# A feed-forward stage in token blocks of 848, 848 and 416 instead of three of 704

## The chip, the cores and the metric

The kernel runs on one core of a Trainium2 chip. The metric is the device time of one execution in microseconds, the median of several runs. One core has TensorE (PE; its weight loads are PEld), VectorE (DVE), ScalarE (ACT), GpSimd (POOL), SyncE (SP, which here only issues transfers) and 16 DMA engines.

## The reference

One layer of a streaming encoder in float32, for 2048 prompt frames and 64 decoder frames of width 1024 (2112 tokens): a projection, two kinds of banded attention, an output projection with a residual, and then the part that matters here:

```python
def conv_ffn(h, conv_state, w_gate_up, conv_w, conv_b, w_down):
    gate, up = jnp.split(jnp.einsum("bsd,df->bsf", h, w_gate_up), 2, axis=-1)   # d = 1024, f = 2816
    ext = jnp.concatenate([conv_state, gate], axis=1)     # two rows of state ahead
    conv = conv_b
    for i in range(3):
        conv = conv + conv_w[i] * ext[:, i:i + t]
    y = jax.nn.silu(conv) * up
    return jnp.einsum("bsf,fd->bsd", y, w_down), ext[:, -2:]
# x = x + conv_ffn(RMSNorm(x)), for the prompt with zero state, for the decoder frames with theirs
```

## The kernel before

Four stages follow each other, with a barrier between: `project`, `attend`, `combine` (output projection, residual x1T and normed input h2T, both to DRAM) and `ffn` (L1413). Only `ffn` is touched. In it the 2112 tokens are columns of the moving operand, in N_BLOCKS = 3 blocks of BLOCK = 704, each cut in SUBS = 2 chunks of SUB = 352. The decoder's 64 tokens are the last columns of the last block; CUT is the column of that block where the prompt ends.

**Precision.** Every float32 operand is split in a hi and a lo part, and `dense` (L74) makes three matmuls for each tile of the contraction: hi x hi, lo x hi, hi x lo. The weights, which are stationary, are split here too: ScalarE copies w_raw to w_hi (`split_hi`, L1580), VectorE subtracts to w_lo (`split_lo`, L1639). Each of the two slots s has one buffer of w_raw, w_hi and w_lo. SyncE refills w_raw (`load_pair`, L1476) as soon as `split_lo` has read it; `split_hi` waits until TensorE has used the old weights (`z_ok[s]` of the slot's last chunk), and TensorE waits for `w_lo_ok[s]`.

**Order.** For each block the 2816 hidden channels come in PARTS = 2 parts. A part has KF = 11 gate/up pairs and then DOWN = 4 down pairs. A gate/up pair has slot 0 for a gate tile and slot 1 for the up tile of the same 128 channels, each with 8 contraction tiles; a down pair has two output tiles with 11 contraction tiles each. A group is what one slot does for one chunk: 8 x 3 = 24 or 11 x 3 = 33 matmuls into z[s][j]. TensorE's order (`pair`, L1550) is slot 0 chunk 0, slot 0 chunk 1, slot 1 chunk 0, slot 1 chunk 1.

**Gate and up.** ScalarE copies z[0][j] to `gate` (L1600), splits the next gate weights, then makes silu of both chunks and splits the next up weights. VectorE (`gate_up`, L1663) copies the two carried columns ahead, convolves each chunk in three operations (`convolve`, L1652, into c1, with c2 between), in the last block also the decoder's 64 columns with their own state (L1675 to L1682), then makes w_lo of slot 0, then for each chunk y = silu x z[1][j] and its hi and lo parts (L1690 to L1695), then w_lo of slot 1. In `down` it adds z to the residual tile acc.

**Between blocks.** In the down pairs of part 1, ScalarE makes h_hi of the next block and POOL h_lo (`split_h`, L1509) from tiles that POOL loads; POOL also stores yT and then loads the next acc. TensorE waits for POOL's eight tiles ahead of a block (L1562). Only for the first block SyncE loads h (into acc, L1486), ScalarE makes h_hi, and VectorE h_lo (L1646); TensorE's first group waits for these tile by tile (L1567).

Of the kernel before, what the change touches and what calls it, by code (L numbers as in the profile page):

```python
# [1412 lines left out]
def ffn(nc, h2T, x1T, w_gu, w_dn, conv, state, yT, gate_prompt, gate_sample):  # L1413
# [10 lines left out]
    LAST = N_BLOCKS - 1  # L1424
    CUT = SEQ - LAST * BLOCK
    H = 2
    with ExitStack() as ctx:
# [15 lines left out]
        y = [m.sbuf(f"y{j}", [P, SUB]) for j in range(SUBS)]  # L1443
# [58 lines left out]
        @block.gpsimd  # L1502
        def _(pool):
            def load_h(b, k):
                if b > 1 or k > 1:
                    pool.wait_ge(p_lo_ok, KD * (b - 1) + k - 1)
                pool.dma_start(h_raw[k % 2][:], h2T[k, :, b * BLOCK:(b + 1) * BLOCK]).then_inc(h_ld[k % 2], 16)

            def split_h(b):  # L1509

                for k in range(KD):
                    n = KD * (b - 1) + k
                    pool.wait_ge(h_hi_ok, n + KD + 1)
                    nc.gpsimd.tensor_tensor(h_lo[:, k, :], h_raw[k % 2][:], h_hi[:, k, :].bitcast(F32), ALU.subtract)\
# [12 lines left out]
            load_acc(0)  # L1527
            for b in range(N_BLOCKS):
                if b < LAST:
                    load_h(b + 1, 0)  # L1530
                    load_h(b + 1, 1)
                    split_h(b + 1)
                g1 = (b * PARTS + PARTS - 1) * PAIRS + KF
                for d in range(KD):
                    for j in range(SUBS):
                        pool.wait_ge(z_free[d % 2][j], g1 + d // 2 + 1)  # L1536
                    pool.dma_start(yT[d, :, b * BLOCK:(b + 1) * BLOCK], acc[:, d, :]).then_inc(y_st, 16)  # L1537
                if b < LAST:
                    load_acc(b + 1)
            pool.wait_ge(carry_ok, N_BLOCKS * F_TILES)  # L1540
            pool.wait_ge(tail_ok, F_TILES)  # L1541
            pool.dma_start(gate_sample, carry[:]).then_inc(gate_st, 16)  # L1542
            pool.dma_start(gate_prompt, tail[:]).then_inc(gate_st, 16)  # L1543
            pool.wait_ge(gate_st, 32)
            pool.wait_ge(y_st, 16 * KD * N_BLOCKS)


        @block.tensor
        def _(pe):
            def pair(g, hi, lo, n_k, ready=None):  # L1550
                for s in range(2):
                    pe.wait_ge(w_lo_ok[s], g + 1)
                    for j in range(SUBS):
                        pe.wait_ge(z_free[s][j], g)
                        cols = slice(j * SUB, (j + 1) * SUB)
                        dense(nc, z[s][j][:, 0:SUB], (lambda k: w_hi[s][:, k, :], lambda k: w_lo[s][:, k, :]),
                              (lambda k: hi[:, k, cols], lambda k: lo[:, k, cols]), n_k,
                              ready and (lambda k: ready(s, j, k))).then_inc(z_ok[s][j], 1)

            for b in range(N_BLOCKS):  # L1560
                if b:
                    pe.wait_ge(p_lo_ok, KD * b)  # L1562
                for part in range(PARTS):
                    n = b * PARTS + part
                    g0 = n * PAIRS
                    if n == 0:
                        pair(0, h_hi, h_lo, KD, lambda s, j, k: s == j == 0 and pe.wait_ge(h_lo_ok, k + 1))  # L1567
                    with pe.Fori(1 if n == 0 else 0, KF) as i:
                        pair(g0 + i, h_hi, h_lo, KD)
                    for j in range(SUBS):  # L1570
                        pe.wait_ge(y_lo_ok[j], KF * (n + 1) - 1)
                    pair(g0 + KF, y_hi, y_lo, KF,
                         lambda s, j, k: k == KF - 1 and s == 0 and pe.wait_ge(y_lo_ok[j], KF * (n + 1)))
                    with pe.Fori(1, DOWN) as i:
                        pair(g0 + KF + i, y_hi, y_lo, KF)
# [3 lines left out]
        def _(act):  # L1579
            def split_hi(s, g, n_k):  # L1580
                act.wait_ge(w_ld[s], 16 * (g + 1))
                act.wait_ge(z_ok[s][1], g)
                nc.scalar.activation(w_hi[s][:, 0:n_k, :], w_raw[s][:, 0:n_k, :], ACT.Copy).then_inc(w_hi_ok[s], 1)  # L1583

            def split_h(b, k):
                if b == 0:
                    act.wait_ge(h0_ld[k], 16)
                    src = acc[:, k, :]
                else:
                    act.wait_ge(h_ld[k % 2], 16 * ((KD * (b - 1) + k) // 2 + 1))  # L1590
# [21 lines left out]
            split_hi(1, 0, KD)
            for b in range(N_BLOCKS):
                for part in range(PARTS):
# [23 lines left out]
        def _(dve):  # L1638
# [24 lines left out]
            def gate_up(b, g, f, c, jf, n_k):  # L1663
# [5 lines left out]
                for j in range(SUBS):  # L1669
# [3 lines left out]
                    convolve(c1[j][:, 0:n], c2[j][:, 0:n], gate[:, j * SUB:H + (j + 1) * SUB], taps, n, c,  # L1673
                             (c1_ok[j], c2_ok[j], conv_ok[j] if n == SUB else s_gate_ok))
# [9 lines left out]
                nc.vector.tensor_scalar(of(carry, f), gate[:, BLOCK:H + BLOCK], 1.0, None, ALU.mult).then_inc(carry_ok, 1)  # L1684
                for j in range(SUBS):
# [4 lines left out]
                    nc.vector.tensor_tensor(y[j][:], silu[j][:], z[1][j][:, 0:SUB], ALU.mult).then_inc(z_free[1][j], 1)  # L1690
                    dve.wait_ge(z_free[1][j], g + 1)
                    hi, lo = (ap[:, ds(jf, 1), cols].rearrange("p a n -> p (a n)") for ap in (y_hi, y_lo))
                    nc.vector.tensor_scalar(hi, y[j][:], 1.0, None, ALU.mult).then_inc(y_hi_ok[j], 1)
                    dve.wait_ge(y_hi_ok[j], c + 1)
                    nc.vector.tensor_tensor(lo, y[j][:], hi.bitcast(F32), ALU.subtract).then_inc(y_lo_ok[j], 1)  # L1695
                split_lo(1, g + 1, n_k)

            def down(g, i, n_k):
                for s in range(2):
                    for j in range(SUBS):  # L1700
                        dve.wait_ge(z_ok[s][j], g + 1)
                        part = acc[:, ds(2 * i + s, 1), j * SUB:(j + 1) * SUB].rearrange("p a n -> p (a n)")
                        nc.vector.tensor_tensor(part, part, z[s][j][:, 0:SUB], ALU.add).then_inc(z_free[s][j], 1)  # L1703
# [11 lines left out]
            for b in range(N_BLOCKS):  # L1715
                for part in range(PARTS):
# [6 lines left out]
                    with nc.vector.Fori(0, DOWN - 1) as i:  # L1723
                        down(g0 + KF + i, i, KF)
                    down(g0 + PAIRS - 1, DOWN - 1, KD if n + 1 < N_BLOCKS * PARTS else 0)
# [98 lines left out]
```

## Time and profile before

| | |
|---|---|
| three runs | 2729.56, 2730.96, 2731.3 us; median 2730.96 |
| the profiled execution | 2730.9 us, its span 2729.1 us |
| mean granted TensorE clock | 0.978 |
| PE busy, share of the span | 2604.4 us, 95% |
| DVE, ACT, POOL busy | 1376.9, 887.8, 189.9 us |
| `ffn` on TensorE | 9504 matmuls of 128x352, from 1203.00 us on |

A row of the timeline gives start, duration, engine, line, operation, tile written and tiles read, shape and count, and in brackets the idle time before it with what ended it. A matmul's duration there is that of its way through the array and overlaps the next one's, so the distance between the starts is what one costs.

### The profile page before, as it was taken

The numbers are of one execution on the slowest core, as the hardware profiler recorded it, in microseconds if no ns is written. First come the engines' busy times: TensorE is split into PE (matmuls) and PEld (weight loads), VectorE is DVE, ScalarE is ACT, GpSimd is POOL, SyncE is SP. The second block draws the span as 40 slices with busy tenths as digits, with TensorE's granted clock in tenths as the row PEclk, the third lists the DMA queues.
The fourth block names the chain that finished last, engine by engine and source line by source line (L and its number), as shares of the span: only waits on it lengthen the run. The fifth ranks groups of instructions, "written<-read, shape, count | busy, mean of one in ns | idle before, by whom it ended". The sixth has DMA issues, their size and how long they took to land.

```text
span 2729.1 us, 45154 instructions
## 1 busy us (share of the span) xinstructions
PE 2604.4 (95%) x16553; PEld 2504.4 (92%) x16553; DVE 1376.9 (50%) x2973; ACT 887.8 (33%) x1696; POOL 189.9 (7%) x125
## 2 busy tenths in 40 slices
PE   6999999589999979969999999999999999999998
PEld 3888888489999979859999999999999999999998
DVE  5544444466667645565534552554355346625651
ACT  4233332476777633232212221221122222212220
POOL 0000000332322200000000002000000210000000
PEclk8999999799999989979999999999999999999999
DMA  6232231544334165562221223322122342221221
GB/s 218 86 96 79 92 94 48 123 114 102 86 86 101 46 236 180 192 238 66 73 75 55 69 92 121 123 69 79 60 69 71 105 145 65 79 68 62 69 87 64
DMA packets 175286, 271.61 MB, mean 100 GB/s; under 512 B 19138, under 2 KB 120482, under 8 KB 175074
## 3 DMA queue, kind: packets, MB, share of 16 engines
q1 hardware_dynamic: 167842, 246.13, 29.8%
q0 software_dynamic: 4848, 23.12, 2.4%
q10 hardware_dynamic: 2512, 1.26, 0.2%
q8 instruction: 51, 0.84, 0.1%
q14 instruction: 33, 0.27, 0.0%
HBM read 216.35 MB, written 55.69 MB: 100 GB/s over the span
## 4 chain that ended last, share of the span: by engine, by line
PE 55%; DVE 0%; DMA 0%; POOL 0%; issue 0%; ACT 0%; SPq 0%; POOLq 0%
PE ffn_z L81 55%; DVE ffn_h_lo L1646 0%; DMA ffn_acc<-h2T_scratch 0%; ACT ffn_h_hi L1592 0%; POOL yT L1537 0%; POOL gate_sample L1542 0%; DVE ffn_acc L1703 0%; POOL gate_prompt L1543 0%; SPq L1488 0%; SPq L1486 0%; POOLq L1541 0%; POOLq L1536 0%
## 5 line engine op out<-in xcount | busy, mean ns | idle before, releaser
L81 PE MATMUL ffn_z<-ffn_h_hi,ffn_w_hi 128*128 128x352 f32 x2112 | 680.6, 322 | 22.1 <-DVE ffn_w_lo L1641 21.9
L81 PE MATMUL ffn_z<-ffn_h_lo,ffn_w_hi 128*128 128x352 f32 x2112 | 680.2, 322 | 0.0
L81 PE MATMUL ffn_z<-ffn_h_hi,ffn_w_lo 128*128 128x352 f32 x2112 | 680.0, 322 | 0.0
L1583 ACT ACTIVATE ffn_w_hi<-ffn_w_raw 128x1024 fp32r<-128x1024 f32 (+1 forms) x180 | 205.6, 1142 | 716.9 <-PE ffn_z L81 715.8
L81 PEld LDWEIGHTS ffn_z<-ffn_h_hi,ffn_w_hi 128*128 128x128 f32 x2112 | 397.2, 188 | 24.2 <-DVE ffn_w_lo L1641 23.0
L81 PEld LDWEIGHTS ffn_z<-ffn_h_hi,ffn_w_lo 128*128 128x128 f32 x2112 | 397.5, 188 | 0.0
L81 PEld LDWEIGHTS ffn_z<-ffn_h_lo,ffn_w_hi 128*128 128x128 f32 x2112 | 397.5, 188 | 0.0
L81 PE MATMUL ffn_z<-ffn_y_lo,ffn_w_hi 128*128 128x352 f32 x1056 | 340.0, 322 | 0.0
L81 PE MATMUL ffn_z<-ffn_y_hi,ffn_w_hi 128*128 128x352 f32 x1056 | 339.7, 322 | 0.0
L81 PE MATMUL ffn_z<-ffn_y_hi,ffn_w_lo 128*128 128x352 f32 x1056 | 339.5, 321 | 0.0
L242 PE MATMUL project_z<-project_w_hi,project_h_hi 128*128 128x512 f32 (+3 forms) x680 | 255.3, 375 | 13.0 <-DVE project_w_lo L411 12.9
L1641 DVE TENSOR_TENSOR ffn_w_lo<-ffn_w_raw,ffn_w_hi 128x1024 fp32r<-128x1024 f32 (+1 forms) x180 | 238.9, 1327 | 37.3 <-ACT ffn_w_hi L1583 37.3
L242 PE MATMUL project_z<-project_w_lo,project_h_hi 128*128 128x512 f32 (+3 forms) x680 | 251.9, 371 | 0.0
L242 PE MATMUL project_z<-project_w_hi,project_h_lo 128*128 128x512 f32 (+3 forms) x680 | 251.9, 370 | 0.0
L836 PE MATMUL attend_o<-attend_v,attend_prob_t 128*128 (+1 forms) x1680 | 222.9, 276 | 0.0
L1703 DVE TENSOR_TENSOR ffn_acc<-ffn_acc,ffn_z 128x352 f32 (+1 forms) x96 | 50.1, 522 | 342.1 <-PE ffn_z L81 342.1
L836 PEld LDWEIGHTS attend_o<-attend_v,attend_prob_t 128*128 128x128 f32 x1680 | 209.6, 193 | 0.6
L81 PEld LDWEIGHTS ffn_z<-ffn_y_hi,ffn_w_lo 128*128 128x128 f32 x1056 | 198.8, 188 | 0.0
L81 PEld LDWEIGHTS ffn_z<-ffn_y_lo,ffn_w_hi 128*128 128x128 f32 x1056 | 198.3, 188 | 0.0
L81 PEld LDWEIGHTS ffn_z<-ffn_y_hi,ffn_w_hi 128*128 128x128 f32 x1056 | 198.1, 188 | 0.0
L1600 ACT ACTIVATE ffn_gate<-ffn_z 128x352 f32<-128x352 f32 x132 | 61.6, 466 | 397.0 <-PE ffn_z L81 396.9
L1654 DVE TENSOR_SCALAR ffn_c<-ffn_gate,ffn_conv 128x352 f32<-128x352 f32 (+1 forms) x132 | 60.5, 458 | 218.7 <-ACT ffn_gate L1600 194.3
(149 smaller groups left out, 3790.8 us busy)
## 6 DMA issues: line engine op xcount, KB each, us to landing
ffn_w_raw<-w_gu SPq DMA_DIRECT2D x132, 512.0 KB, 3.6
ffn_w_raw<-w_dn SPq DMA_DIRECT2D x48, 704.0 KB, 4.1
combine_w_raw<-w_o SPq DMA_DIRECT2D x24, 512.0 KB, 4.9
combine_o_raw<-oT_scratch SPq DMA_DIRECT2D x12, 704.0 KB, 6.4
combine_x<-xT SPq DMA_DIRECT2D x12, 704.0 KB, 7.4
x1T_scratch<-combine_x SPq DMA_DIRECT2D x12, 704.0 KB, 7.5
ffn_acc<-x1T_scratch POOLq DMA_DIRECT2D x3, 2816.0 KB, 11.8
yT<-ffn_acc POOLq DMA_DIRECT2D x24, 352.0 KB
```

Source lines behind the costliest of these rows:

```text
L81: last = nc.tensor.matmul(out, w_parts[w](k), act_parts[a](k), start=(k == 0 and (w, a) == PASSES[0]), stop=(k == n_k - 1 and (w, a) == PA ...
L242: last = nc.tensor.matmul(z[c][0:w, 0:width], h[:, k, 0:w], ww[:, k, first:first + width], start=(k == 0 and h is hi and ww is w_hi), stop ...
L836: last = nc.tensor.matmul(o_ps[u % 2][:, head * P:(head + 1) * P], prob_t[u % 2][:, src:src + P], v[:, ds(tile + j, 1), pair * P:(pair + 1 ...
L1583: nc.scalar.activation(w_hi[s][:, 0:n_k, :], w_raw[s][:, 0:n_k, :], ACT.Copy).then_inc(w_hi_ok[s], 1)
L1600: nc.scalar.activation(gate[:, H + j * SUB:H + (j + 1) * SUB], z[0][j][:, 0:SUB], ACT.Copy)\
L1641: nc.vector.tensor_tensor(w_lo[s][:, 0:n_k, :], w_raw[s][:, 0:n_k, :], w_hi[s][:, 0:n_k, :].bitcast(F32), ALU.subtract).then_inc(w_lo_ok[s ...
L1654: nc.vector.tensor_scalar(dst, src[:, H:H + n], taps[:, 2:3], taps[:, 3:4], ALU.mult, ALU.add)\
L1703: nc.vector.tensor_tensor(part, part, z[s][j][:, 0:SUB], ALU.add).then_inc(z_free[s][j], 1)
```

## The change

In `ffn` alone SUB is 424 and BLOCK 848: the first two blocks have two chunks of 424, the last has REST = 416 tokens in a single chunk 0. `subs(b)` gives (index, first column, width) of a block's chunks. Every loop over chunks, every tile width and the columns of every transfer follow it. The tile y goes: it lies in c2 now, and a wait of VectorE for its own y_lo_ok stands ahead of the convolution. In the last block the prompt's convolution has CUT = 352 columns, the decoder's 64 stand behind it in the same chunk, and VectorE's `split_lo(0)` comes between the two. The other stages keep 704 and 352. The core of the diff:

```diff
+    SUB, SUBS = 424, 2
+    BLOCK = SUB * SUBS
+    REST = TOKENS - LAST * BLOCK
     CUT = SEQ - LAST * BLOCK
+    def subs(b):
+        return ((0, 0, SUB), (1, SUB, SUB)) if b < LAST else ((0, 0, REST),)
+    def cols_of(b):
+        return slice(b * BLOCK, min((b + 1) * BLOCK, TOKENS))
+    def wide(b):
+        return BLOCK if b < LAST else REST
...
-        y = [m.sbuf(f"y{j}", [P, SUB]) for j in range(SUBS)]
...
-                pool.dma_start(acc[:], x1T[:, :, b * BLOCK:(b + 1) * BLOCK].rearrange("k p n -> p k n"))\
+                pool.dma_start(acc[:, :, 0:wide(b)], x1T[:, :, cols_of(b)].rearrange("k p n -> p k n"))\
...
-            def pair(g, hi, lo, n_k, ready=None):
+            def pair(b, g, hi, lo, n_k, ready=None):
                 for s in range(2):
                     pe.wait_ge(w_lo_ok[s], g + 1)
-                    for j in range(SUBS):
+                    for j, at, width in subs(b):
                         pe.wait_ge(z_free[s][j], g)
-                        cols = slice(j * SUB, (j + 1) * SUB)
+                        cols = slice(at, at + width)
...
-            def split_hi(s, g, n_k):
+            def split_hi(b, s, g, n_k):
                 act.wait_ge(w_ld[s], 16 * (g + 1))
-                act.wait_ge(z_ok[s][1], g)
+                act.wait_ge(z_ok[s][subs(b)[-1][0]], g)
...
-                for j in range(SUBS):
+                for j, at, width in subs(b):
                     dve.wait_ge(z_free[0][j], g + 1)
                     dve.wait_ge(silu_ok[j], c)
-                    n = CUT - j * SUB if b == LAST and j else SUB
+                    dve.wait_ge(y_lo_ok[j], c)
+                    n = CUT if b == LAST else width
...
                 if b == LAST:
+                    split_lo(0, g + 1, n_k)
                     cs = c - LAST * F_TILES
                     nc.vector.tensor_scalar(gate_s[:, 0:H], of(state_sb, f), 1.0, None, ALU.mult).then_inc(s_gate_ok, 1)
-                    nc.vector.tensor_scalar(gate_s[:, H:], gate[:, H + CUT:], 1.0, None, ALU.mult).then_inc(s_gate_ok, 1)
+                    nc.vector.tensor_scalar(gate_s[:, H:], gate[:, H + CUT:H + REST], 1.0, None, ALU.mult).then_inc(s_gate_ok, 1)
                     dve.wait_ge(s_gate_ok, 3 * cs + 3)
-                    n = CUT - SUB
-                    convolve(c1[1][:, n:], c2[1][:, n:], gate_s, taps, DEC, cs, (s1_ok, s2_ok, conv_ok[1]))
+                    convolve(c1[0][:, CUT:REST], c2[0][:, CUT:REST], gate_s, taps, DEC, cs, (s1_ok, s2_ok, conv_ok[0]))
                     nc.vector.tensor_scalar(of(tail, f), gate[:, CUT:H + CUT], 1.0, None, ALU.mult).then_inc(tail_ok, 1)
-                split_lo(0, g + 1, n_k)
+                if b < LAST:
+                    split_lo(0, g + 1, n_k)
...
-                for j in range(SUBS):
-                    cols = slice(j * SUB, (j + 1) * SUB)
+                for j, at, width in subs(b):
+                    cols = slice(at, at + width)
+                    y = c2[j][:, 0:width]
                     dve.wait_ge(silu_ok[j], c + 1)
                     dve.wait_ge(z_ok[1][j], g + 1)
-                    dve.wait_ge(y_lo_ok[j], c)
```

## Rows read from the trace of the kernel before

**Rows 1.** The page, its span line.
```profile
span 2729.1 us, 45154 instructions
```

**Rows 2.** The chain that ended last, in order of time: start us, us, what.
```profile
1209.54 1510.53 PE ffn_z L81 x9483
...
2720.09 0.53 DVE ffn_acc L1703
```

**Rows 3.** Waits from 1196 us on: total us, times, longest.
```profile
PE ffn_z L81 <- DVE ffn_w_lo L1641: 21.9, 1, 21.9
```

**Rows 4.** Last block, part 1: length; busy PE PEld DVE ACT POOL; clock; DMA share, GB/s.
```profile
2467.62:2719.73 252.11, 252.11 (x1585) 252.11 (x1584) 122.95 (x265) 52.01 (x73) 3.81 (x7) 1.00 0.22 73
```

**Rows 5.** Timeline of PE: first matmuls of groups, slot 0; then a down group.
```profile
2498.18 0.32 PE L81 MATMUL ffn_z<-ffn_h_hi,ffn_w_hi 128*128 128x352 f32 x1
...
2502.02 0.32 PE L81 MATMUL ffn_z<-ffn_h_hi,ffn_w_hi 128*128 128x352 f32 x1
...
2505.82 0.32 PE L81 MATMUL ffn_z<-ffn_h_hi,ffn_w_hi 128*128 128x352 f32 x1
```
```profile
2414.99 0.32 PE L81 MATMUL ffn_z<-ffn_y_hi,ffn_w_hi 128*128 128x352 f32 x1
...
2420.30 0.32 PE L81 MATMUL ffn_z<-ffn_y_hi,ffn_w_hi 128*128 128x352 f32 x1
```

**Rows 6.** Timeline of PE in the projection, 24 matmuls of 512 apart.
```profile
252.12 0.39 PE L242 MATMUL project_z<-project_w_hi,project_h_hi 128*128 128x512 f32 x1
...
257.56 0.39 PE L242 MATMUL project_z<-project_w_hi,project_h_hi 128*128 128x512 f32 x1
```

**Rows 7.** Timeline of ACT and DVE at the start of the stage.
```profile
1202.46 6.11 ACT L1592 ACTIVATE ffn_h_hi<-ffn_acc 128x704 fp32r<-128x704 f32 x7 [0.78 <-DMA ffn_acc<-h2T_scratch]
1209.16 1.06 ACT L1583 ACTIVATE ffn_w_hi<-ffn_w_raw 128x1024 fp32r<-128x1024 f32 x1 [0.59 <-DMA ffn_w_raw<-w_gu]
...
1203.28 6.21 DVE L1646 TENSOR_TENSOR ffn_h_lo<-ffn_acc,ffn_h_hi 128x704 fp32r<-128x704 f32 x7 [0.34 <-ACT ffn_h_hi L1592]
```

**Rows 8.** Groups by form from 1196 us on: busy us, mean ns; idle before.
```profile
L1641 DVE TENSOR_TENSOR ffn_w_lo<-ffn_w_raw,ffn_w_hi 128x1408 fp32r<-128x1408 f32 x48 | 78.0, 1625 | 29.6 <-ACT ffn_w_hi L1583 29.6
...
L1583 ACT ACTIVATE ffn_w_hi<-ffn_w_raw 128x1408 fp32r<-128x1408 f32 x48 | 66.3, 1380 | 348.7 <-PE ffn_z L81 348.7
```

**Rows 9.** Timeline of DVE in one gate/up pair of the last block.
```profile
2503.05 0.47 DVE L1654 TENSOR_SCALAR ffn_c<-ffn_gate,ffn_conv 128x352 f32<-128x352 f32 x1 [1.73 <-ACT ffn_gate L1600]
2503.67 0.58 DVE L1657 SCALAR_TENSOR_TENSOR ffn_c<-ffn_gate,ffn_conv,ffn_c 128x352 f32<-128x352 f32 x1 [0.15 <-DVE ffn_c L1654]
2504.40 0.58 DVE L1660 SCALAR_TENSOR_TENSOR ffn_c<-ffn_gate,ffn_conv,ffn_c 128x352 f32<-128x352 f32 x1
...
2507.97 0.16 DVE L1677 TENSOR_SCALAR ffn_gate_s<-ffn_state 128x2 f32 x1
...
2508.94 0.28 DVE L1660 SCALAR_TENSOR_TENSOR ffn_c<-ffn_gate_s,ffn_conv,ffn_c 128x64 f32<-128x64 f32 x1
...
2509.21 1.22 DVE L1641 TENSOR_TENSOR ffn_w_lo<-ffn_w_raw,ffn_w_hi 128x1024 fp32r<-128x1024 f32 x1
2510.35 0.16 DVE L1684 TENSOR_SCALAR ffn_carry<-ffn_gate 128x2 f32 x1
2510.42 0.51 DVE L1690 TENSOR_TENSOR ffn_y<-ffn_silu,ffn_z 128x352 f32<-128x352 f32 x1
...
2511.55 0.53 DVE L1695 TENSOR_TENSOR ffn_y_lo<-ffn_y,ffn_y_hi 128x352 f32 x1
```

**Rows 10.** Timeline of ACT in the same pair.
```profile
2502.30 0.47 ACT L1600 ACTIVATE ffn_gate<-ffn_z 128x352 f32<-128x352 f32 x1 [2.81 <-PE ffn_z L81]
...
2509.26 0.50 ACT L1605 ACTIVATE ffn_silu<-ffn_c 128x352 f32<-128x352 f32 x1 [1.44 <-DVE ffn_c L1660]
```

**Rows 11.** The page's DMA issues: KB each, us to landing.
```profile
ffn_w_raw<-w_gu SPq DMA_DIRECT2D x132, 512.0 KB, 3.6
```

**Rows 12.** Timeline of POOL, its last tile splits for the last block.
```profile
2196.72 4.14 POOL L1514 TENSOR_TENSOR ffn_h_lo<-ffn_h_raw,ffn_h_hi 128x704 fp32r<-128x704 f32 x2 [15.13 <-ACT ffn_h_hi L1592]
```

More of the change, by code:

```diff
@@ L1513, in split_h @@
                     pool.wait_ge(h_hi_ok, n + KD + 1)
-                    nc.gpsimd.tensor_tensor(h_lo[:, k, :], h_raw[k % 2][:], h_hi[:, k, :].bitcast(F32), ALU.subtract)\
+                    nc.gpsimd.tensor_tensor(h_lo[:, k, 0:wide(b)], h_raw[k % 2][:, 0:wide(b)], h_hi[:, k, 0:wide(b)].bitcast(F32), ALU.subtract)\
                         .then_inc(p_lo_ok, 1)
@@ L1534, in _ @@
                 for d in range(KD):
-                    for j in range(SUBS):
+                    for j, _, _ in subs(b):
                         pool.wait_ge(z_free[d % 2][j], g1 + d // 2 + 1)
-                    pool.dma_start(yT[d, :, b * BLOCK:(b + 1) * BLOCK], acc[:, d, :]).then_inc(y_st, 16)
+                    pool.dma_start(yT[d, :, cols_of(b)], acc[:, d, 0:wide(b)]).then_inc(y_st, 16)
                 if b < LAST:
@@ L1566, in _ @@
                     if n == 0:
-                        pair(0, h_hi, h_lo, KD, lambda s, j, k: s == j == 0 and pe.wait_ge(h_lo_ok, k + 1))
+                        pair(b, 0, h_hi, h_lo, KD, lambda s, j, k: s == j == 0 and pe.wait_ge(h_lo_ok, k + 1))
                     with pe.Fori(1 if n == 0 else 0, KF) as i:
-                        pair(g0 + i, h_hi, h_lo, KD)
-                    for j in range(SUBS):
+                        pair(b, g0 + i, h_hi, h_lo, KD)
+                    for j, _, _ in subs(b):
                         pe.wait_ge(y_lo_ok[j], KF * (n + 1) - 1)
-                    pair(g0 + KF, y_hi, y_lo, KF,
+                    pair(b, g0 + KF, y_hi, y_lo, KF,
                          lambda s, j, k: k == KF - 1 and s == 0 and pe.wait_ge(y_lo_ok[j], KF * (n + 1)))
                     with pe.Fori(1, DOWN) as i:
-                        pair(g0 + KF + i, y_hi, y_lo, KF)
+                        pair(b, g0 + KF + i, y_hi, y_lo, KF)
         @block.scalar
         def _(act):
-            def split_hi(s, g, n_k):
+            def split_hi(b, s, g, n_k):
                 act.wait_ge(w_ld[s], 16 * (g + 1))
-                act.wait_ge(z_ok[s][1], g)
+                act.wait_ge(z_ok[s][subs(b)[-1][0]], g)
                 nc.scalar.activation(w_hi[s][:, 0:n_k, :], w_raw[s][:, 0:n_k, :], ACT.Copy).then_inc(w_hi_ok[s], 1)
@@ L1590, in split_h @@
                     act.wait_ge(h_ld[k % 2], 16 * ((KD * (b - 1) + k) // 2 + 1))
-                    src = h_raw[k % 2][:]
-                nc.scalar.activation(h_hi[:, k, :], src, ACT.Copy).then_inc(h_hi_ok, 1)
+                    src = h_raw[k % 2][:, 0:wide(b)]
+                nc.scalar.activation(h_hi[:, k, 0:wide(b)], src, ACT.Copy).then_inc(h_hi_ok, 1)
             def gate_up(b, g, c, n_k):
-                for j in range(SUBS):
+                for j, at, width in subs(b):
                     act.wait_ge(z_ok[0][j], g + 1)
@@ L1668, in gate_up @@
                 dve.wait_ge(halo_ok, c + 1)
-                for j in range(SUBS):
+                for j, at, width in subs(b):
                     dve.wait_ge(z_free[0][j], g + 1)
                     dve.wait_ge(silu_ok[j], c)
-                    n = CUT - j * SUB if b == LAST and j else SUB
-                    convolve(c1[j][:, 0:n], c2[j][:, 0:n], gate[:, j * SUB:H + (j + 1) * SUB], taps, n, c,
-                             (c1_ok[j], c2_ok[j], conv_ok[j] if n == SUB else s_gate_ok))
+                    dve.wait_ge(y_lo_ok[j], c)
+                    n = CUT if b == LAST else width
+                    convolve(c1[j][:, 0:n], c2[j][:, 0:n], gate[:, at:H + at + width], taps, n, c,
+                             (c1_ok[j], c2_ok[j], conv_ok[j] if n == width else s_gate_ok))
@@ L1685, in gate_up @@
-                for j in range(SUBS):
-                    cols = slice(j * SUB, (j + 1) * SUB)
+                if b < LAST:
+                    split_lo(0, g + 1, n_k)
+                nc.vector.tensor_scalar(of(carry, f), gate[:, wide(b):H + wide(b)], 1.0, None, ALU.mult).then_inc(carry_ok, 1)
+                for j, at, width in subs(b):
+                    cols = slice(at, at + width)
+                    y = c2[j][:, 0:width]
                     dve.wait_ge(silu_ok[j], c + 1)
                     dve.wait_ge(z_ok[1][j], g + 1)
-                    dve.wait_ge(y_lo_ok[j], c)
-                    nc.vector.tensor_tensor(y[j][:], silu[j][:], z[1][j][:, 0:SUB], ALU.mult).then_inc(z_free[1][j], 1)
+                    nc.vector.tensor_tensor(y, silu[j][:, 0:width], z[1][j][:, 0:width], ALU.mult).then_inc(z_free[1][j], 1)
@@ L1696, in gate_up, with down @@
                 split_lo(1, g + 1, n_k)
-            def down(g, i, n_k):
+            def down(b, g, i, n_k):
                 for s in range(2):
-                    for j in range(SUBS):
+                    for j, at, width in subs(b):
                         dve.wait_ge(z_ok[s][j], g + 1)
-                        part = acc[:, ds(2 * i + s, 1), j * SUB:(j + 1) * SUB].rearrange("p a n -> p (a n)")
-                        nc.vector.tensor_tensor(part, part, z[s][j][:, 0:SUB], ALU.add).then_inc(z_free[s][j], 1)
+                        part = acc[:, ds(2 * i + s, 1), at:at + width].rearrange("p a n -> p (a n)")
+                        nc.vector.tensor_tensor(part, part, z[s][j][:, 0:width], ALU.add).then_inc(z_free[s][j], 1)
@@ L1723, in _ @@
                     with nc.vector.Fori(0, DOWN - 1) as i:
[L1724 to L1725 removed]
+                        down(b, g0 + KF + i, i, KF)
+                    down(b, g0 + PAIRS - 1, DOWN - 1, KD if n + 1 < N_BLOCKS * PARTS else 0)
 def encoder_step(nc, a):
```

35 lines of the change are left out of this document (17 added, 18 removed).

## Prediction, made before the changed kernel ran

> **What bounds the kernel now.** I began with the page's span line, then the chain of waits, because a change to one stage is worth only what it takes off that chain. The span is 2729.1 us [rows 1]; the profiled execution took 2730.9 us, so 1.8 us lie around the span, and it stands 0.06 us under the median of the three runs (2730.96). The reader should see in the chain [rows 2] that from 1209.54 us on, one piece of 1510.53 us is TensorE working on ffn_z with nothing between, and that only vector and store work of a few us follows. The waits of TensorE in this stage [rows 3] show one idle stretch, the 21.9 us before its first matmul. Within a part of the stage (11 gate/up pairs, 4 down pairs) TensorE is busy for all 252.11 us, the granted clock is 1.00, which is 2.4 GHz, while VectorE has 122.95 us of work, ScalarE 52.01 and the DMA engines 22% [rows 4]. So the stage is matmul instructions one behind the other, and only their number and their spacing (pitch) count.
>
> **Pitch.** A group of 24 matmuls of 352 columns takes 3.84 us in chunk 0 (160.0 ns each) and 3.80 us in chunk 1 (158.3 ns); the 33 of a down group with the second weight slot take 5.31 us (161.1 ns, the dearest I found) [rows 5]. Over a part, 252.11 us / 1584 = 159.2 ns. In the projection 24 matmuls of 512 columns take 5.44 us, 226.7 ns [rows 6]. Between 160.0 and 226.7 lie 160 columns: 0.417 ns a column, one column a cycle of the 2.4 GHz clock. What is left, 160.0 - 146.7 = 13.3 ns and 226.7 - 213.3 = 13.3 ns, is the same at both widths: a price per instruction. In the groups of the feed-forward stage it runs from 11.6 (chunk 1) to 14.4 ns (that down group), 12.6 on average, by where the operands lie.
>
> **Matmuls, removed.** Per weight tile there were six chunks, now five: 9504 matmuls become 7920 (6336 of 424 columns, 1584 of 416), and the columns stay 3,345,408, at 0.4167 ns 1393.9 us. Before: 1393.9 + 9504 x 12.6 ns = 1513.6 us. After, bounded by the cheapest mean (12.6) and the dearest group (14.4): 1493.7 and 1508.0 us. I take 13.1 ns, nearest to what both widths show in chunk 0: the last block has only a chunk 0, and the second chunk now starts at column 424, where I don't know whether it keeps the discount of chunk 1, so I give it half. That makes 1497.7 us: **-15.9 us**, bounds -19.9 and -5.6.
> The Trainium skill (TensorE: Matmul & The Clock Gate, section "Wait — 56ns, not 53.3ns?") speaks against this change: it has only about 2.5 ns as the fixed cost of a matmul at full clock. By that page the removal of 1584 instructions would give an estimated 4.0 us. The rows above show 13.3 ns at two widths, so the measurement decides here.
>
> **Start of the stage, lengthened.** Before the last of the first group's eight steps TensorE waits for the eight h_lo tiles. ScalarE's seven h_hi tiles run without a gap from 1202.46 on, VectorE's seven h_lo from 1203.28 in 6.21 us, 0.887 us each [rows 7]. Each tile now has 848 columns. VectorE's subtraction of 1408 columns takes 1.625 us and of 1024 columns 1.22 us [rows 8, 9], 1.06 ns a column, so 0.15 us more for each of 144 columns: 7 x 0.15 = 1.1 us. The run starts later too: the transfers are saturated here (until the second weight tile is split at 1209.16 [rows 7], eight tiles of 352 KB and two weight tiles of 512 KB, 3.84 MB, in some 12.5 us, 0.31 MB a us), two tiles of 72 KB more are 0.46 us, and ScalarE's copy of 144 columns more about 0.12. Sum 1.7; the later tiles need 576 KB more in all, 1.9 us. I take **+1.8 us**, between 1.0 (the clock is up earlier in the group) and 2.6 (transfers bound it).
>
> **The last block, with one chunk.** In the wide blocks each group of 24 lasts 4.55 us instead of 3.8 and all chains get longer cover than before. In the last block the two weight slots alternate every T = 24 x 186.7 ns = 4.48 us, where a slot's two chunks gave 7.64. Two chains start when TensorE ends the gate group (0); all steps are from [rows 9, 10], widened by 64 columns at 1.06 ns (VectorE) and, from 1.38 and 1.06 us for the same widths [rows 7, 8], 0.85 ns (ScalarE):
> To the gate weights: ScalarE's gate copy starts 0.28 after the group (2502.02 to 2502.30); the convolution starts 0.75 + 0.05 later; first to third operation 1.35 (the prompt's part of this block has 2048 - 1696 = 352 columns, just these rows); the third occupies the queue 0.50; split_lo, moved here ahead of the decoder's part, 1.22, and 0.05 to TensorE. Sum 4.20, needed at 4.48: cover 0.28.
> To the up weights: 2.93 as above, 1.14 for split_lo, 0.97 from the state copy to the last small operation, 0.32 until silu, 0.59 for silu and the step to VectorE, 1.23 from y to y_lo, 0.52 for y_lo, 1.22 for the second split_lo, 0.05: 8.97, needed at 2T = 8.96. No cover. A chain longer than 2T costs TensorE half of the overrun in each pair: the up group starts late, but the gate group before it, which starts the next chain, has ended on time. VectorE sits idle 0.15 us between some dependent operations (at 2503.67 [rows 9]); one to three more such gaps would make an overrun of up to 0.45 us, half of it in 22 pairs 5 us. In the last pair of each part the moved split_lo has 11 tiles, 1625 ns, and is 0.12 us late, twice. Together I take **+2.0 us**, bounds 0 and 5.
> The weight load of a slot is issued when split_lo has read it, at 4.20 for the gate slot; it lands 3.6 us later [rows 11] and is wanted at 2T + 0.6 = 9.6: hidden, 1.7 us to spare, of which some goes where the residual tile is loaded. In down groups (33 x 186.7 = 6.16 us) the chain is 0.28 + 1.38 + 1.63, 3.3 us: hidden.
>
> **The rest at nothing.** y in c2, and the wait for y_lo ahead of the convolution: VectorE itself raised that count a pair earlier. The small state, tail and carry copies keep their number; moving split_lo ahead of them delays only conv_ok, counted above. POOL splits the next block's tiles in the last down pairs; its last two operations start at 2196.72 and take 4.14 us, while the last block begins one part ahead of 2467.62, at 2215.4 [rows 4, 12]. At 848 columns they take 5.0 us and the cover of 14 us becomes longer. POOL's stores and SyncE's loads are as many as before. At the end the last addition is 0.07 us wider and the last store is 208 KB instead of 352: nothing. Losing such a cover would cost what it covers, 5 us for POOL's two operations.
>
> **Sum.** 2730.9 - 15.9 + 1.8 + 2.0 = 2718.8 us, said as 2719.
>
> **Rivals.** A measurement can tell about 0.2%, 5.5 us, from no change.
> (1) The last block starves: VectorE's single chain overruns by 0.8 to 1.3 us instead of 0.2. Price 9 to 14 us for 22 pairs, so 2726 to 2731. For it: there is no second chunk to interleave, and my chain has no cover. Against: its steps come from the same instructions; I know of no further one. Chance 0.10, of which 0.07 within 0.2% of before.
> (2) Slower, by one mechanism: where the moving operand lies. The second chunk begins 1696 bytes into a row instead of 1408, and rows are 3392 bytes instead of 2816. If the 424-column matmuls cost more per instruction than the dearest group now, the gain turns: from 15.9 ns on (190.0 ns pitch becomes 192.6) it is 5.5 us slower than before. At 20 ns a matmul: 6336 x 6.9 ns = 43.7 us over my sum, 2762. For it: the pitch does move with the chunk and with the weight slot by up to 2.8 ns [rows 5]. Against: those are all the differences that other offsets and tiles make. Chance 0.06.
> (3) The extra over the columns goes with the columns (12.6 ns per 352) and not with the instruction. Then nothing is saved: 2730.9 + 3.8 = 2734.7, most likely within 0.2%. Against: 13.3 ns at 352 and at 512. Chance 0.04. By the page's rule cited above, the Trainium skill would put the sum at an estimated 2730.7.
> Forecast case: 0.80, its own range 2712 (the discount of chunk 1 kept, no stall) to 2725 (pitch of 14 ns or a full 5 us of stall). The range of 8 in 10 is nearly that; I end it at 2712 and 2726.
> Chances: faster 0.80 + 0.03 of (1) = 0.83; within 0.2%: 0.07 of (1) + 0.03 of (3) = 0.10; slower: 0.06 of (2) + 0.01 of (3) = 0.07.
>
> **What the changed profile would show.** The chain's TensorE piece starts near 1211.3 us and has some 7,900 matmuls. Groups of 24 in the wide blocks last 4.52 to 4.56 us; a part of a wide block lasts about 300 us (1584 matmuls at 189.8 ns), one of the last block 147 to 149 us. In the last block TensorE's waits should name ffn_w_lo, 22 to 24 times, with 0.1 us each; 0.5 us each is rival 1. For 128x424 a pitch over 192 ns is rival 2 (rival 3 would give 159.2 x 424 / 352 = 191.8). If TensorE idles at a block's start, the tile split on POOL or the residual load was not hidden, and I was wrong on the covers.

## The result and the profile after

The changed kernel takes 2738.59 us (median of 10 runs, 2736.22 to 2742.07), the one before 2731.25 us in the runs beside it (10 runs, 2727.68 to 2733.93): a ratio of 1.0026, 95% interval 1.0017 to 1.0035. The forecast was 2719 us, 12 us faster; it came out 7 us slower. The profiled execution took 2737.9 us.

The changed kernel's page, its span line, which answers to [rows 1]:

```profile
span 2736.1 us, 41704 instructions
```

Its chain of waits in order of time (start us, us, what), which answers to [rows 2]:

```profile
1211.49 1509.79 PE ffn_z L81 x7866
...
2721.30 0.60 DVE ffn_acc L1719
```

The piece that was 1510.53 us for 9483 matmuls is 1509.79 us for 7866. It starts 1.95 us later, and the last group of 33 isn't in it: the chain passes from the group before it, by VectorE's addition, to POOL's stores, while TensorE goes on to 2727.2 us. From the first to the last matmul of the stage it is 1522.7 us against 1516.7 us. TensorE's waits in the stage (us, times, longest) beside [rows 3]:

```profile
PE ffn_z L81 <- DVE ffn_w_lo L1655: 22.5, 1, 22.5
...
PE ffn_z L81 <- DVE ffn_h_lo L1660: 0.2, 1, 0.2
```

So nothing took the place of the removed matmuls as a wait. Busy time by stretch, answering to [rows 4]: a part of a wide block, then the two parts of the last block (length; PE, PEld, DVE, ACT, POOL; clock; DMA share, GB/s):

```profile
1817.97:2123.17 305.20, 305.20 (x1585) 297.48 (x1584) 124.04 (x200) 55.81 (x74) 2.54 (x4) 1.00 0.22 71
...
2428.38:2577.81 149.43, 149.43 (x793) 147.69 (x792) 91.96 (x192) 43.72 (x52) 1.45 (x2) 1.00 0.41 130
2577.81:2727.15 149.34, 149.34 (x792) 147.45 (x792) 90.77 (x191) 42.67 (x51) 3.80 (x7) 1.00 0.36 116
```

At the full clock, 1584 matmuls of 424 columns take 305.2 us where 300.6 were forecast: 192.7 ns each, 16.0 above the columns at 2.4 GHz. The last block's take 188.7 ns, 15.4 above. That is where the time went. TensorE's timeline shows it in single groups: first matmuls of a gate group and the next two, 24 apart, then of a down group and the next, 33 apart:

```profile
2215.40 0.35 PE L81 MATMUL ffn_z<-ffn_h_hi,ffn_w_hi 128*128 128x424 f32 x1
...
2220.00 0.35 PE L81 MATMUL ffn_z<-ffn_h_hi,ffn_w_hi 128*128 128x424 f32 x1
...
2224.62 0.35 PE L81 MATMUL ffn_z<-ffn_h_hi,ffn_w_hi 128*128 128x424 f32 x1
...
2332.38 0.36 PE L81 MATMUL ffn_z<-ffn_y_hi,ffn_w_hi 128*128 128x424 f32 x1
...
2338.78 0.36 PE L81 MATMUL ffn_z<-ffn_y_hi,ffn_w_hi 128*128 128x424 f32 x1
```

4.60 us / 24 is 191.7 ns, 4.62 us is 192.5, 6.40 us / 33 is 193.9 ns (195.2 in most down groups of chunk 1, 192.7 in those of chunk 0), against 160.0, 158.3 and 161.1 in [rows 5]. Most groups of a kind repeat their matmul distances to a nanosecond or two, so this is not chance.

### The profile page after: what moved, and what is told of

Same layout as the page of the kernel before. It is cut to its first block, busy times and chain, and to the rows that moved or that the text cites. A ratio compares the mean times of both kernels' runs of the same rounds, so it can differ in the third digit from the quotient of the medians.

```text
span 2736.1 us, 41704 instructions
## 1 busy us (share of the span) xinstructions
PE 2609.3 (95%) x14969; PEld 2475.0 (90%) x14969; DVE 1351.3 (49%) x2825; ACT 880.0 (32%) x1652; POOL 188.0 (7%) x125
## 4 chain that ended last, share of the span: by engine, by line
PE 55%; DVE 0%; issue 0%; DMA 0%; POOL 0%; ACT 0%; SPq 0%; POOLq 0%
PE ffn_z L81 55%; DVE ffn_h_lo L1660 0%; DMA ffn_w_raw<-w_gu 0%; DVE ffn_w_lo L1655 0%; POOL yT L1550 0%; ACT ffn_w_hi L1597 0%; DVE ffn_acc L1719 0%; POOL gate_prompt L1556 0%; POOL gate_sample L1555 0%; SPq L1499 0%; POOLq L1554 0%
## 5 line engine op out<-in xcount | busy, mean ns | idle before, releaser
L81 PE MATMUL ffn_z<-ffn_h_hi,ffn_w_hi 128*128 128x424 f32 (+1 forms) x1760 | 622.3, 354 | 22.7 <-DVE ffn_w_lo L1655 22.5
L81 PE MATMUL ffn_z<-ffn_h_lo,ffn_w_hi 128*128 128x424 f32 (+1 forms) x1760 | 623.9, 354 | 0.0
L81 PE MATMUL ffn_z<-ffn_h_hi,ffn_w_lo 128*128 128x424 f32 (+1 forms) x1760 | 622.9, 354 | 0.0
L81 PEld LDWEIGHTS ffn_z<-ffn_h_hi,ffn_w_hi 128*128 128x128 f32 x1760 | 331.4, 188 | 33.4 <-DVE ffn_w_lo L1655 23.5
L81 PEld LDWEIGHTS ffn_z<-ffn_h_lo,ffn_w_hi 128*128 128x128 f32 x1760 | 331.0, 188 | 6.4
L81 PEld LDWEIGHTS ffn_z<-ffn_h_hi,ffn_w_lo 128*128 128x128 f32 x1760 | 331.1, 188 | 6.1
L81 PE MATMUL ffn_z<-ffn_y_hi,ffn_w_lo 128*128 128x424 f32 (+1 forms) x880 | 312.9, 356 | 0.0
L81 PE MATMUL ffn_z<-ffn_y_lo,ffn_w_hi 128*128 128x424 f32 (+1 forms) x880 | 312.4, 355 | 0.0
L81 PE MATMUL ffn_z<-ffn_y_hi,ffn_w_hi 128*128 128x424 f32 (+1 forms) x880 | 311.8, 354 | 0.0
L242 PE MATMUL project_z<-project_w_hi,project_h_hi 128*128 128x512 f32 (+3 forms) x680 | 255.2, 375 | 14.8 <-DVE project_w_lo L411 14.8
L1614 ACT ACTIVATE ffn_gate<-ffn_z 128x424 f32<-128x424 f32 (+1 forms) x110 | 57.7, 524 | 386.7 <-PE ffn_z L81 386.7
```

The lines of the kernel that those rows point to most:

```text
L81: last = nc.tensor.matmul(out, w_parts[w](k), act_parts[a](k), start=(k == 0 and (w, a) == PASSES[0]), stop=(k == n_k - 1 and (w, a) == PA ...
L242: last = nc.tensor.matmul(z[c][0:w, 0:width], h[:, k, 0:w], ww[:, k, first:first + width], start=(k == 0 and h is hi and ww is w_hi), stop ...
L1614: nc.scalar.activation(gate[:, H + at:H + at + width], z[0][j][:, 0:width], ACT.Copy)\
```

## The experiments

Called "stage" below: the six block parts, first matmul to first matmul, with 252.27 us each before (1513.6 us), the first one's start-up loss of 3 us left out; in the changed kernel 4 x 305.2 + 149.4 + 149.5 = 1519.8 us. Executions of one kernel differ by several us (the kernel before took 2726.4 to 2734.3 us over all its runs), and the first matmul of the stage starts between 1200 and 1207 us, so where a kernel ran once I go by its stage. Its length repeats: 1513.6 us in the kernel before and in e11_shift128 alike. "Extra" is a matmul's distance to the next less its columns at 0.4167 ns.

**Narrower chunks, with rows 64 bytes shorter.**

```diff
-    SUB, SUBS = 424, 2
+    SUB, SUBS = 416, 2
```
(c1, c2 and silu of chunk 0 are then 448 wide for the last block.)

> Blocks of 832, 832 and 448 (chunks 416, 416; 448): the same five chunks and 7920 matmuls, rows of 3328 bytes instead of 3392, second chunk at byte 1664 instead of 1696. Theory place (the price above the columns comes from where the rows of the moving operand start; rows of 3328 = 26 x 128 bytes with a chunk at 13 x 128 are of the kind of the kernel before, 22 x 128 and 11 x 128): pitch 186.7 ns in chunk 0 and 185 ns in chunk 1 of the wide blocks, 200 ns in the last, TensorE's stage 1494 to 1500 us, time 2714 to 2719 us. Rival width (416 and 424 columns themselves cost 15 to 16 ns above the columns instead of 13): pitch 188.5 to 189.5 ns in the wide blocks, stage about 1512 us, time 2729 to 2732 us.

2735.42 us, ratio 1.0020 (1.0011 to 1.0030) to the kernel before: slower too. Stretches of a wide part and of the last block's first:

```profile
2105.98:2404.78 298.80, 298.80 (x1585) 296.05 (x1584) 122.98 (x200) 59.19 (x82) 20.24 (x21) 1.00 0.22 73
2404.78:2565.29 160.51, 160.51 (x793) 148.74 (x793) 94.00 (x192) 44.28 (x52) 1.45 (x2) 1.00 0.38 122
```

Chunk 0 costs 188.0 ns in the mean of gate/up and down groups, chunk 1 189.2, the 448 columns 202.7: extras of 14.7, 15.9 and 16.0. Place as I had put it, in multiples of 128 bytes, doesn't bring 13.3 back. The stage is 1516.3 us.

**The same chunks, rows 3392 bytes apart.** h_hi, h_lo, y_hi and y_lo are allocated with 848 columns a row.

> As e1_sub416, but the rows of the h and y tiles stay 848 columns (3392 bytes) apart, 16 columns of each unused. Theory place with the row distance as its cause: pitch 188.3 to 189.2 ns in all groups of 416 columns, as in the changed kernel's last block, so a wide part of 1584 matmuls takes 299 us instead of 295. If only the second chunk's start matters: chunk 0 at 186.7 ns. Rival width: the same pitches as e1_sub416.

Stage 1516.2 us, the same as above; 188.8 and 188.1 ns in the gate/up groups' two chunks, 189.5 and 188.8 in the down groups'. At 416 columns the row distance does nothing to the sum: it makes chunk 0 1.0 ns dearer and chunk 1 0.8 ns cheaper.

**The kernel before, rows 3392 bytes apart.**

```diff
-        h_hi = m.sbuf("h_hi", [P, KD, BLOCK], F32R)
+        h_hi = m.sbuf("h_hi", [P, KD, 848], F32R)
```
(and so h_lo, y_hi, y_lo)

> The kernel before, with the rows of the h and y tiles 848 columns (3392 bytes) apart, chunks of 352 as they were: the row distance alone. Theory place: the pitch of 352-column matmuls rises from 158.3 to 161.1 to about 162 to 163 ns in all groups, a part of 1584 takes 257 to 258 us instead of 252.3, the time rises by 28 to 34 us to about 2762. Rival width: no change, 2731 us.

```profile
1714.67:1968.44 253.77, 253.77 (x1585) 253.77 (x1585) 114.59 (x200) 53.09 (x74) 2.52 (x4) 1.00 0.26 84
```

1.5 us a part more, less than a third of what was expected; stage 1522.6 us, 2740.66 us in one run. At 352 columns the row distance costs 0.9 ns a matmul, by taking chunk 1's 158.3 ns away (159.9 in its gate/up groups, 161.2 in its down groups). It isn't nothing, and isn't the cause of 16.0.

**Weights moved by 64 bytes** (the changed kernel with a tile of 16 words ahead of w_raw).

> The changed kernel with 64 unused bytes ahead of the weight tiles, so that only the weights' place against the rows of the moving operand moves. If the price comes from the meeting of weight load and moving read in certain places, the order of dear and cheap matmuls in a group changes and the mean pitch (192.7 ns in the wide blocks) moves by 1 ns or more. If it comes from the moving rows alone: the same 192.7 ns and the same pattern, 2738 us.

305.7 us a part instead of 305.2, but another order inside a group: chunk 0 rises from 191.7 to 193.2 ns, down groups of chunk 1 fall from 195.2 to 193.4. Where the weights lie matters to single matmuls; the mean moved by 0.3 ns, so neither expectation holds as it stood. Changing a row distance also moves the weight tiles behind the rows, by far more than 64 bytes; no run here moves the weights alone as far.

**Widths, measured in place.** Only TensorE's width changes; columns are left out or repeated.

```diff
+            W0, W1 = [256, 320, 384, 512, 480, 416], [352, 360, 376, 408, 0, 0]
...
+                        if n is not None:
+                            width = (W0, W1)[j][n]
```

> A measurement, not a version: the changed kernel, but TensorE's groups are 256, 320, 384, 512, 480, 416 columns wide in chunk 0 of the six block parts (after the very first pair) and 352, 360, 376, 408 in chunk 1 of the first four, so it leaves out or repeats columns. Theory width: the price above the columns depends on the number of columns: 13.3 ns at 256 and 512 as in the projection, 12.6 to 13.5 at 352, 15 to 18 at 416 and above 400 in general, whatever the chunk. Theory row distance (rows of 3392 bytes): 512 and 256 columns cost 15 ns or more here, where the projection, with rows of 9216 bytes, has 13.3. Rival threshold: from some width between 352 and 416 on everything is dearer, 480 and 512 too (16 ns).

> The same measurement with 288, 336, 400, 448, 432, 368 columns in chunk 0 and 256, 320, 392, 384 in chunk 1. Theory width: 448 as in the last block of e1_sub416 (202.7 ns, 16.0 above the columns), chunk 0 and chunk 1 within 1 ns of each other at 256, 320 and 384. If where the chunk starts decides instead: the two chunks differ by more than the widths do.

With rows of 3392 bytes the extra climbs with the columns (the table below): 12.0 ns at 256, 19.2 at 512, where the projection's 512 columns cost 13.3. None of the guesses fits whole: 512 is not as cheap as in the projection, 256 not dear, and there is no threshold. Between groups of a kind, chunk 0 and chunk 1 differ by about 1 ns at 256, 320 and 384 columns, less than the widths. A line of 4.4 ns a matmul and 0.444 ns a column meets these points to 1 ns: from 256 to 512 columns, in these rows, a column costs more than the clock's 0.417. The 368 columns of e6_sweep_b's last part are left out of the table, because TensorE waited there (see the last block, below).

**Five chunks of other widths.**

```diff
-    SUB, SUBS = 424, 2
-    BLOCK = SUB * SUBS
+    SUB, SUB1, SUBS = 512, 288, 2
+    BLOCK = SUB + SUB1
...
-        return ((0, 0, SUB), (1, SUB, SUB)) if b < LAST else ((0, 0, REST),)
+        return ((0, 0, SUB), (1, SUB, SUB1)) if b < LAST else ((0, 0, REST),)
```

> Five chunks of other widths: blocks of 800 (chunks of 512 and 288), 800 and 512. Theory width, with 13.3 ns at 256 and 512: the sum over the five chunks is 880 + 67 = 946.7 ns instead of 955.6 before, TensorE's stage 14 us shorter than before, time about 2717 us. If rows of 3200 bytes or widths above 400 cost 16 ns: at least 9 us more than that, 2726 to 2730 us.

2739.59 us, ratio 1.0038 (1.0024 to 1.0052). 288 columns cost 133.3 ns in the gate/up groups, but 512 cost 232.2 and 230.1, an extra of 18.9 and 16.8. That is dearer than either expectation had it: the stage is 1521.9 us.

**The same, gate/up rows 3584 bytes apart** (h_hi and h_lo with 896 columns, 256 unused bytes ahead).

> e7_512_288 with the rows of the h tiles 896 columns (3584 bytes) apart and 256 unused bytes ahead of them, so that in gate/up groups every row starts at the same place of a 512-byte frame, as in the projection; the y tiles (down groups) stay as they were. Theory frame (a matmul costs 13.3 ns above its columns where all rows start at one place of the frame): gate/up groups of 512 columns fall from 232.2 to 226.7 ns, down groups stay at 230.1, a wide part 286.2 us instead of 288.8. Theory rate (in this stage a column costs 0.444 ns and a matmul 4.4 ns, and the frame moves it by 1 ns or so): 231 to 233 ns stay.

Groups of 512 fall to 228.7 ns in the wide blocks and to 226.7 in the last; down groups, whose rows stayed, keep 230.1 and 229.9. Stage 1504.7 us, 2722.5 us in one run. So how the h tiles lie decides what 512 columns cost. The edit changes their row distance, their start by 256 bytes and with both their distance from the weights; The row distance is the likeliest of these, because a shift of all starts does nothing at 352 columns (e11_shift128, below), but no run shows it alone. In the wide blocks the first ten or so matmuls of a group stayed dear (224 to 236 ns each); then came 226, 227, 227 and so on. They are dear where a chunk of 288 columns went before; in the last block, where 512 follow 512, none is.

**Widths in the projection.** PE's chunks there are 448, 224, 416, 384, 480 wide from the third token tile on, which leaves columns of the projection out.

> A measurement: the changed kernel, whose projection has groups of 448, 224, 416, 384 and 480 columns from the third token tile on instead of 512, 256, 512, 512, 512; it leaves columns of the projection out. Theory rate as a thing of the feed-forward stage alone: columns / 2.4 GHz + 13.3 ns at all widths here: 200.0, 186.7, 173.3 and 213.3 ns. Theory width (some numbers of columns are dear anywhere): 448, 416, 384 and 480 cost 15 to 18 ns above the columns, as in e5 and e6, and only 256 and 512 cost 13.3.

TensorE's timeline, a group of 448 and one of 416 columns, 15 matmuls from the first row of each pair to the second:

```profile
224.90 0.36 PE L244 MATMUL project_z<-project_w_hi,project_h_lo 128*128 128x448 f32 x1
...
227.94 0.36 PE L244 MATMUL project_z<-project_w_hi,project_h_lo 128*128 128x448 f32 x1
...
233.21 0.35 PE L244 MATMUL project_z<-project_w_hi,project_h_lo 128*128 128x416 f32 x1
...
236.03 0.35 PE L244 MATMUL project_z<-project_w_hi,project_h_lo 128*128 128x416 f32 x1
```

3.04 us / 15 is 202.7 ns, 2.82 / 15 is 188.0: extras of 16.0 and 14.7 (14.8 over all such groups), and 16.4 at 480, but 13.3 at 384 and, in the kernels before and after, at 512. The 224 columns of this run, about which nothing was expected, cost 111.6 ns, an extra of 18.2: narrow isn't cheap as such. The number of columns is a cause by itself, in another stage with other rows.

**Widths in the places of the kernel before.**

> A measurement: the kernel before, all tiles where they are (rows of 2816 bytes), but TensorE's groups 256, 320, 384, 416, 448, 512 columns wide in chunk 0 of the six block parts and 256, 288, 304, 320, 336, 352 in chunk 1 (after the very first pair); it leaves out or repeats columns. Theory place: with the row distance of before all widths cost 11.6 to 13.3 ns above the columns, 416 columns 186.7 ns. Theory rate (a column costs more than 0.417 ns): 416 columns 188 to 190 ns, 512 columns 231 to 233 ns here too, 256 columns 118 to 119.

TensorE's timeline in groups of 416 and 512 columns, 23 matmuls apart: 188.3 and, before rounding of the starts, 227.7 ns (the first five, which follow a chunk of 352 columns, take 228 to 236, the others 226.7). So neither theory holds as a whole: 416 columns cost what the rate gives, 512 do not, and 256 cost 119.7.

```profile
1950.40 0.35 PE L81 MATMUL ffn_z<-ffn_h_hi,ffn_w_hi 128*128 128x416 f32 x1
...
1954.73 0.35 PE L81 MATMUL ffn_z<-ffn_h_hi,ffn_w_lo 128*128 128x416 f32 x1
...
2509.82 0.39 PE L81 MATMUL ffn_z<-ffn_h_hi,ffn_w_hi 128*128 128x512 f32 x1
...
2515.05 0.39 PE L81 MATMUL ffn_z<-ffn_h_hi,ffn_w_lo 128*128 128x512 f32 x1
```

> The measurement of e10_sweep_704 with 424, 408, 400, 432, 368 and 392 columns in chunk 0 and 264, 272, 296, 312, 328, 344 in chunk 1, in the places of the kernel before. If the number of columns makes 424 dear by itself, it costs 15 ns or more above the columns here as well (192 ns); if the row distance of 3392 bytes does it all, 13.3 (190.0 ns), as I predicted for the changed kernel. 368 and 344 lie among widths that cost 13.3 (320, 336, 352, 384): if they are dearer, multiples of 32 are what is cheap, and 416 and 448 are exceptions to that.

Groups of 424 columns, weight slot 0 and slot 1, 23 matmuls apart:

```profile
1280.39 0.36 PE L81 MATMUL ffn_z<-ffn_h_hi,ffn_w_hi 128*128 128x424 f32 x1
...
1284.77 0.35 PE L81 MATMUL ffn_z<-ffn_h_hi,ffn_w_lo 128*128 128x424 f32 x1
...
1287.84 0.36 PE L81 MATMUL ffn_z<-ffn_h_hi,ffn_w_hi 128*128 128x424 f32 x1
...
1292.29 0.35 PE L81 MATMUL ffn_z<-ffn_h_hi,ffn_w_lo 128*128 128x424 f32 x1
```

190.4 and 193.5 ns; the down groups of the two slots 192.5 and 193.5. Weighted as in a part, 424 columns have an extra of 15.7 ns in chunk 0 with rows of 2816 bytes; in the changed kernel chunk 0 has 15.4 and chunk 1 16.6. Extras in ns, chunk 0, weighted means of gate/up and down groups ("-": not measured; the projection's row holds the repeating part of a group):

| columns | 256 | 320 | 352 | 384 | 400 | 408 | 416 | 424 | 432 | 448 | 480 | 512 |
|---|---|---|---|---|---|---|---|---|---|---|---|---|
| rows of 2816 bytes | 13.1 | 13.3 | 13.5 | 14.1 | 13.7 | 15.0 | 15.0 | 15.7 | 16.2 | 15.5 | - | 14.2 |
| rows of 3392 bytes | 12.0 | 13.0 | 13.5 | 14.9 | 15.4 | - | 15.4 | 15.4 | 16.1 | 16.2 | 17.8 | 19.2 |
| projection, 9216 bytes | 13.3 | - | - | 13.3 | - | - | 14.8 | - | - | 16.0 | 16.4 | 13.3 |

The guess that multiples of 32 columns are cheap falls: 416 and 448 are dear, 400 isn't, and in the same run 368 cost 13.4 and 392 14.1 in chunk 0, and 312 in chunk 1 only 10.5.

**All tiles 128 bytes later** (the kernel before, a tile of 32 words ahead of h_hi).

> The kernel before with 128 unused bytes ahead of the h tiles, so that all tiles behind them start 128 bytes later. If the start of a row within 256 bytes decides between 160.0 ns (chunk 0) and 158.3 ns (chunk 1), the two swap and the time stays at 2731 us. If only distances between operands count: nothing changes. If it is neither, both move.

Nothing moved: 160.0, 158.3 and 161.1 ns in the same groups. The absolute start of a row isn't what counts, at least by 128 bytes and at 352 columns; what differs between kernels are distances and widths.

**Both avoided.** Chunks of 512 and 288, 512 and 288, 512, with rows of h and y 3328 bytes (832 columns) apart.

> e7_512_288 (five chunks, 512 and 288, 512 and 288, 512) with the rows of the h and y tiles 832 columns (3328 = 6.5 x 512 bytes) apart, as 2816 is 5.5 x 512. Theory of two causes (number of columns and row distance): 512 columns at 226.7 to 227 ns and 288 at 133.3, TensorE's stage 7920 matmuls in 1500 us, 14 us under the kernel before, time 2716 to 2719 us. If 3328 is as bad as 3200: 232 ns and 2738 us.

2716.66 us, ratio 0.9946 (0.9932 to 0.9959): faster than both kernels, 13.9 us under the kernel before of the same runs, with as many matmuls as the change. A wide part and the last block's first part:

```profile
1778.11:2063.11 285.00, 285.00 (x1586) 252.83 (x1585) 120.93 (x200) 54.74 (x74) 2.52 (x4) 1.00 0.23 76
2348.11:2527.65 179.54, 179.54 (x794) 148.65 (x793) 98.05 (x192) 45.45 (x52) 1.45 (x2) 1.00 0.34 111
```

Stage 1499.1 us; 512 columns cost 226.7 to 228.7 ns, 288 cost 131.6. Stage and time are as expected, in part by luck: in the wide blocks 512 columns cost 1.6 ns more than expected (228.3 in the mean) and 288 cost 1.7 ns less.

## Why the prediction was wrong

**The step that failed** is the price in "Matmuls, removed": 13.1 ns above the columns for the new widths, between bounds of 12.6 and 14.4. It measured 16.0 ns at 424 and 15.4 at 416 columns, outside both bounds. That is 6336 x 2.9 + 1584 x 2.3 ns = 22.0 us, more than the forecast's miss (2737.9 - 2718.8 = 19.1 us); the added terms for the start and the last block, which did not come (below), make up the difference. The span grew by 7.0 us: 6.2 in the stage, 1.4 ahead of its first matmul, less 0.2 in the first part's start-up loss and 0.4 in the tail. The price was read at two widths, 352 and 512, and taken for a constant because they agreed; between them it isn't one. By the table, 15.7 of the 16.0 ns come with 424 columns at the old row distance as well (e13_sweep_704b), and 15.0 of the 15.4 at 416: against 13.1 that is 19.5 us for the number of columns, and 2.5 us for the place of the second chunk and the rest. This division rests on chunk 0 alone, since chunk 1 of the old kernel was not measured at 424 columns. So my bounds held all places of the feed-forward stage, but only one width. Why some numbers of columns are dearer stays open.

**Rival 2** had the right sign and size (192.7 ns against its 192.6), and, by that division, the wrong mechanism: where the second chunk starts and how far rows are apart moved the sum by little here. So its number came true by luck. The rows mattered most at 512 columns, by 5 ns (e10_sweep_704 against e5_sweep_a). **Rival 3**, extra with the columns, fits the rows of 3392 bytes best (0.444 ns a column); what I held against it, 13.3 ns at 512, was true of the projection's rows, and in e12_rows832 of rows of 3328 bytes in the last block, but not of rows of 3392. Its 191.8 ns were nearer than my 189.8.

**The Trainium skill's rule** of about 2.5 ns a matmul (TensorE: Matmul & The Clock Gate, section "Wait — 56ns, not 53.3ns?"): no group here shows it. The extra was 10 ns or more throughout, and e12_rows832 gained 14.5 us of stage from 1584 matmuls less, 9 ns for each.

**The last block**: rival 1 didn't happen, and the +2.0 us was too much. The chain in the changed kernel, VectorE's timeline between the end of a gate group at 2609.49 and the next up group at 2618.55 (TensorE):

```profile
2610.57 0.47 DVE L1668 TENSOR_SCALAR ffn_c<-ffn_gate,ffn_conv 128x352 f32<-128x352 f32 x1 [1.14 <-ACT ffn_gate L1614]
...
2612.42 1.22 DVE L1655 TENSOR_TENSOR ffn_w_lo<-ffn_w_raw,ffn_w_hi 128x1024 fp32r<-128x1024 f32 x1
...
2616.17 0.38 DVE L1709 TENSOR_SCALAR ffn_y_hi<-ffn_c 128x416 f32 x1 [0.16 <-DVE ffn_c L1706]
...
2617.18 1.22 DVE L1655 TENSOR_TENSOR ffn_w_lo<-ffn_w_raw,ffn_w_hi 128x1024 fp32r<-128x1024 f32 x1
```

The gate's w_lo is ready at 2613.64, 4.15 us after the group, the up's at 2618.40, 8.91 us after it; with 0.05 to TensorE that is 4.20 and 8.96, forecast 4.20 and 8.97. The pair takes 9.06 us, since the matmuls are dearer than 186.7 ns. So the chain was right and ends just in time, and TensorE's waits show none, where I had forecast 22 to 24 waits of 0.1 us for ffn_w_lo. Up groups of part 1 are 0.6 ns a matmul dearer than gate groups, 0.2 us in all, which is the most that it can have cost: not 2.0 us. e6_sweep_b shows what the chain does when it is too long: with 368 columns in the second part of the last block the two groups of a pair need about 8.0 us, VectorE's work stayed as wide as in the changed kernel, and a gate/up pair took 8.54 us, 0.4 us of it before the up group. That loss of 0.5 us is half of the overrun (8.96 - 8.0 us), as the prediction had it.

**The start**, +1.8 us: the last wait of the first group ends at 1211.49 instead of 1209.54 us, 1.95 later, but 0.87 of that is SyncE's first load of the stage (1197.17 instead of 1196.30), which belongs to the stages ahead. Against later parts, the first part loses 3.1 us (308.35 - 305.21) where it lost 3.3 (255.56 - 252.27). The tiles did come 1.1 us later, forecast 1.7. Half of this, 0.54 us, is there at the first matmul already (it starts 7.24 us after SyncE's first load, 6.70 before); for the other half I had not set against it that the 21 matmuls made while waiting are longer too. That leaves about 0.4 us for the term, which one trace can't tell from nothing: the first part of e11_shift128, a kernel like the one before, lost 5.2 us.

**The covers** (POOL's tile splits, weight loads, the residual load, the wait for y_lo) all held: TensorE has no wait at a block's start or anywhere behind its first group. The tail from TensorE's last matmul to the end of the span is 9.0 us against 9.4.

## What to carry to other kernels

The price of a matmul beyond its columns is not a constant that can be read at two widths and used at a third: here it was 13.5 to 14.2 ns at 352, 384, 400 and 512 columns and 15 to 16 ns from 408 to 448, in the same rows and chunk 0. Before retiling, measure the very widths and the very row distance of the new tiles, for example by changing only TensorE's widths in the old kernel; two such runs gave 15.7 ns at 424 (13.7 to 16.8 by group) and 15.0 at 416. With these the prediction's own sum makes 1517 us of the stage, against 1513.6 before: no gain from fewer, wider matmuls of these widths. Then choose widths and pad rows by that measurement: the same idea with 512 and 288 columns in rows of 3328 bytes gained 0.54% where 424 in rows of 3392 lost 0.26%.

## What the runs showed of the hardware that was not expected

The distance between matmuls depends on the number of columns in steps that I can't derive: about 140 ns for 304 as for 312 columns (chunk 1, rows of 2816 bytes), about 180 for 400 and 188 for 416 (chunk 0). With rows of 3392 bytes a column more costs 0.444 ns between 256 and 512 columns, where a cycle of the 2.4 GHz clock is 0.417 (512 columns in gate/up groups: 232.8 ns with rows of 3392 bytes, 227.8 with 2816). And 512 columns settle at 226.7 ns only after five to ten dearer matmuls where a chunk of 288 or 352 columns went before (e8_rows896, e10_sweep_704, e12_rows832); in the last block of e8_rows896 and e12_rows832, where 512 follow 512, they are cheap from the start. Groups of a kind repeat their pattern, a shift of all tiles by 128 bytes leaves it (in the kernel before), and moving the weights alone by 64 bytes changes it. That weight reads and the reads of the moving rows get into each other's way would fit this, but no run separates them, so why these widths and distances are cheap stays open.
